# Where the softmax division stands in a windowed attention block

## What is computed

```python
s = jnp.einsum('...qhgd,...shd->...hgqs', q, k).astype(jnp.float32) * scale
s = jnp.where(mask[..., None, None, :, :], s, NEG_INF)
m = jnp.maximum(jnp.max(s, axis=-1, keepdims=True), sink)
p = jnp.exp(s - m)
denom = jnp.sum(p, axis=-1, keepdims=True) + jnp.exp(sink - m)
p = (p / denom).astype(v.dtype)
return jnp.einsum('...hgqs,...shd->...qhgd', p, v).astype(q.dtype)
```

## Time and profile before

| | us |
|---|---|
| median of 3 runs (lowest, highest) | 2438.33 (2435.63, 2440.2) |
| the profiled execution, its own time | 2430.51 |
| span of its trace | 2428.8 |
| TensorE busy | 2279.8 (94%) |
| VectorE busy | 1681.7 (69%) |
| ScalarE busy | 983.6 (40%) |
| GpSimd busy | 719.1 (30%) |

### The profile page before, as it was taken

How to read it: one execution, slowest core, us unless ns; L and a number is a source line. 1 busy time by engine, 2 the same in 40 slices (tenths; PEclk the granted TensorE clock), 3 DMA queues, 4 the chain that set the end, 5 groups by cost and what they waited for, 6 DMA issues and landing times.

```text
span 2428.8 us, 36140 instructions
## 1 busy us (share of the span) xinstructions
PE 2279.8 (94%) x14396; PEld 2034.1 (84%) x14396; DVE 1681.7 (69%) x2092; ACT 983.6 (40%) x1773; POOL 719.1 (30%) x396
## 2 busy tenths in 40 slices
PE   7999899699999999999999998987999999999997
PEld 7997577699999998887799876667999999987875
DVE  1579747777777776777536797476777777767676
ACT  3227634533443343343322366344344334443332
POOL 1110134444434440220211102344443444302201
PEclk9999889899999999999999998898999999999999
DMA  5321146122222224765552213451122222255752
GB/s 160 85 51 37 60 132 180 44 82 64 73 82 77 70 72 153 268 207 191 167 129 45 55 37 103 131 159 45 59 79 82 70 72 76 99 216 195 241 198 94
DMA packets 207975, 269.52 MB, mean 111 GB/s; under 512 B 31952, under 2 KB 166584, under 8 KB 207736
## 3 DMA queue, kind: packets, MB, share of 16 engines
q1 hardware_dynamic: 207808, 267.21, 35.9%
HBM read 217.39 MB, written 46.13 MB: 108 GB/s over the span
## 4 chain that ended last, share of the span: by engine, by line
PE 62%; DVE 17%; ACT 6%; issue 5%; POOL 4%; DMA 3%; SPq 2%; DVEq 0%; ACTq 0%; POOLq 0%
PE ps L2014 23%; PE ps L1734 18%; PE ps L1698 8%; PE ps L1956 6%; DMA wblk<-in_w_up 2%; POOL bl L716 2%; POOL wblk L724 1%; ACT bh L908 1%; SPq L529 1%; PE ps L1759 1%; DVE bl L1310 1%; DVE Sb L1524 1%; DVE bnst L1210 1%; DVE rl L1378 1%; PE ps L1853 1%
## 5 line engine op out<-in xcount | busy, mean ns | idle before, releaser
L2014 PE MATMUL ps<-bt,bh 128*128 128x272 f32 x3520 | 598.3, 293 | 29.3 <-issue 19.5
L2014 PEld LDWEIGHTS ps<-bt,bh 128*128 128x128 f32 x3520 | 503.9, 191 | 36.5 <-issue 25.2
L908 ACT ACTIVATE bh<-wblk 128x512 fp32r<-128x512 f32 x308 | 183.6, 624 | 543.1 <-POOL wblk L728 237.4
L2014 PE MATMUL ps<-bt,bl 128*128 128x272 f32 x1760 | 367.8, 291 | 0.0
L1310 DVE TENSOR_TENSOR bl<-wblk,bh 128x512 fp32r<-128x512 f32 x210 | 165.2, 804 | 183.4 <-ACT bh L908 183.4
L2014 PEld LDWEIGHTS ps<-bt,bl 128*128 128x128 f32 x1760 | 278.7, 191 | 0.0
L1734 PE MATMUL ps<-rh,ah 128*128 128x512 f32 (+1 forms) x792 | 246.3, 392 | 13.7 <-DVE rzd L1206 6.8
L716 POOL TENSOR_TENSOR bl<-wblk,bh 128x512 fp32r<-128x512 f32 x98 | 164.7, 1685 | 311.7 <-ACT bh L908 311.7
L2014 PE MATMUL ps<-ba,bh 128*128 128x272 f32 x1408 | 239.9, 293 | 9.1 <-POOL bl L716 4.1
L1734 PE MATMUL ps<-rh,al 128*128 128x512 f32 (+1 forms) x792 | 245.1, 391 | 0.0
L1734 PE MATMUL ps<-rl,ah 128*128 128x512 f32 (+1 forms) x792 | 244.4, 390 | 0.0
(11 more groups left out here) (223 smaller groups left out, 4051.5 us busy)
## 6 DMA issues: line engine op xcount, KB each, us to landing
wrow<-in_w_down SPq DMA_DIRECT2D x132, 512.0 KB, 4.3
wblk<-in_w_up SPq DMA_DIRECT2D x88, 512.0 KB, 5.2
a_scr<-hg SPq DMA_DIRECT2D x44, 552.0 KB, 3.4
araw<-a_scr SPq DMA_DIRECT2D x88, 192.0 KB, 4.1
wrow<-in_w_out SPq DMA_DIRECT2D x48, 256.0 KB, 5.3
wrow<-in_w_out SPq DMA_DIRECT2D x24, 512.0 KB, 3.5
wraw<-in_w_in SPq DMA_DIRECT2D x10, 1024.0 KB, 6.3
z_scr<-rzc SPq DMA_DIRECT2D x16, 512.0 KB, 3.6
```

The source lines that it names most:

```text
L908: act.activation(bh[b][:], block_of(f, b), ACT.Copy).then_inc(S["u_hi"], 1)
L2014: e = nc.tensor.matmul(out[:, n, :], lhs, rhs[:, HW_ // 2 * n:HW_ // 2 * n + HW_ // 2], start=(k == 0 and m == 0), stop=(k == HK - 1 and m ...
```

## The change

The probabilities stay unnormalised: L1524 is gone, `turned` waits for the exponentials alone (`a_exp`), and the product with the values is made with them as they are. The output is put right afterwards. A new function `shares(b)` on TensorE multiplies, for each of the 8 heads, the column of reciprocals (read 64 times over as the stationary operand) by the identity, so that each query's reciprocal stands on the 64 rows of its head, 128x512 in all, in PSUM bank 7. ScalarE still copies the output to `hT`, and a new `o_evac` on VectorE multiplies it there by bank 7. Since bank 7 also takes the turned values, `values_in(b)` now waits for that product of block b - 1, and has moved: it stood one block earlier, as `values_in(b + 1)`, behind the previous block's pieces. After the last block ScalarE copies the output ahead of `m_hi(l, 0)`, and TensorE's transpose of the last keys waits for the last product.

```diff
@@ ScalarE
+                o_evac(NB - 1)
                 m_hi(l, 0)
-                o_evac(NB - 1)
                 m_hi(l, 1)
@@ VectorE
                     dve.wait_ge(S["a_den"], k + 1)
+                    after(dve, "pe_r", l * NB + b)
                     dve.reciprocal(ast[:, 5, hs], ast[:, 5, hs]).then_inc(S["a_rd"], 1)
-                    dve.wait_ge(S["a_rd"], k + 1)
-                    dve.tensor_tensor(Sb[:, hs, :], Sb[:, hs, :], ast[:, 5, hs].unsqueeze(2).to_broadcast([P, 4, 2 * P]), ALU.mult)\
-                        .then_inc(S["a_nrm"], 1)
+                def o_evac(b):
+                    dve.wait_ge(S["a_o"], l * NB + b + 1)
+                    dve.wait_ge(S["pe_r"], l * NB + b + 1)
+                    o = hT[:, T_Q:T_Q + 4, b * P:b * P + P]
+                    dve.tensor_tensor(o, o, ps[:, 7, :].rearrange("p (j q) -> p j q", q=P), ALU.mult).then_inc(S["a_oev"], 1)
...
                     softmax_in(b, 1)
+                    if b:
+                        o_evac(b - 1)
                     dve.wait_ge(S["pe_vtr"], n + 1)
...
                     softmax_out(b, 1)
+                o_evac(NB - 1)
                 m_lo(l, 0)
@@ TensorE
                     after(pe, "a_vr", n)
+                    after(pe, "a_oev", n)
                     pe.transpose(ps[:, 7, 0:P], vst[:], ident[:]).then_inc(S["pe_vtr"], 1)
...
-                    pe.wait_ge(S["a_nrm"], 2 * (l * NB + b) + hf + 1)
+                    pe.wait_ge(S["a_exp"], 2 * (l * NB + b) + hf + 1)
...
-                    after(pe, "a_oev", n)
+                    after(pe, "a_o", n)
...
+                def shares(b):
+                    n = l * NB + b
+                    pe.wait_ge(S["a_rd"], 2 * n + 2)
+                    for kv in range(KV):
+                        o = 64 * kv
+                        for i in range(4):
+                            h = 4 * (i // 2) + 2 * kv + i % 2
+                            e = nc.tensor.matmul(ps[o:o + 64, 7, P * i:P * i + P], ast[:, 5, h:h + 1].to_broadcast([P, HD]), ident[:],
+                                                 start=True, stop=True)
+                    e.then_inc(S["pe_r"], 1)
...
+                    if b:
+                        values_in(b)
                     if b < NB - 1:
-                        values_in(b + 1)
                         scores(b + 1, 0)
                     turned(b, 0)
                     turned(b, 1)
                     if b < NB - 1:
                         scores(b + 1, 1)
                     values(b)
+                    shares(b)
+                pe.wait_ge(S["a_oev"], (l + 1) * NB)
                 pe.transpose(ps[:, 7, P:2 * P], kring[:, (NB - 1) % 2, :], ident[:]).then_inc(S["kv_tr"], 1)
```

More of the change, by code:

```diff
@@ L309, in trunk @@
                   "par_ev wt_tr wt_ev wt_ok wa_landed0 wa_landed1 w_hi w_lo in_done in_ev zu_ev zu_gelu gated "
-                  "g_dve g_pe g_act gv_out k_sw k_rot q_sw0 q_sw1 a_pre a_sm a_max a_m a_neg a_vr a_exp a_den a_rd a_nrm "
-                  "a_ptev a_oev pe_vtr pe_s pe_tr pe_pv kv_tr kv_ev kv_out kvc_landed s_pe s_dve s_act s_out c_out pad_ok "
+                  "g_dve g_pe g_act gv_out k_sw k_rot q_sw0 q_sw1 a_pre a_sm a_max a_m a_neg a_vr a_exp a_den a_rd pe_r "
+                  "a_ptev a_o a_oev pe_vtr pe_s pe_tr pe_pv kv_tr kv_ev kv_out kvc_landed s_pe s_dve s_act s_out c_out pad_ok "
                   "m_hi m_lo wc_landed0 wc_landed1 wc_landed2 wc_landed3 c_hused c_used c_done rz_landed0 rz_landed1 rz_landed2 "
@@ L1043, in o_evac @@
                     act.activation(hT[:, T_Q:T_Q + 4, b * P:b * P + P], ps[:, 6, :].rearrange("p (j q) -> p j q", q=P), ACT.Copy)\
-                        .then_inc(S["a_oev"], 1)
+                        .then_inc(S["a_o"], 1)
                 for b in range(NB):
```

## The result

The changed kernel takes 2490.02 us as the median of four runs (2488.28 to 2494.49), the kernel before 2436.98 beside it (2431.62 to 2440.2). The ratio is 1.0226, 95% interval 1.0214 to 1.0239: slower by 2.3%, or some 55 us. The prediction was 2492 with a range of 2474 to 2510. The profiled execution took 2490.49 us, with a span of 2488.8; before, 2430.51 and 2428.8.

A forecast was written before the change was run, and what follows sets the result against it. With TensorE's and VectorE's near-equal streams bounding the attention stage, and TensorE's path lengthened, 41.5 us for the two layers plus 12.6 for the clock made 54, taking the median from 2438.3 to 2492; range 2474 to 2510.

The forecast's parts named there:

- The bound: Attention stage: TensorE and VectorE both near their limit (97.06 and 98.41 of 112.90 us), TensorE nearly without gaps in block 1.
- The moved step: Blocks 1 to 6, both layers: scores start 2.85 us after the values' transpose starts, formerly 0.20; TensorE loses 2.65 each.
- The shares, 1.02 us a block: Eight small products on TensorE's path in every block, priced at 1.02 us from the gated MLP's eight of that form.
- The other bound: Upper price of the shares: eight full 128x128 operands at the transposes' pace, 1.09 us for four, so 2.18.
- the repeated column is slow: Rival: the shares take 2.18 us instead of 1.02, 18.6 us more in all, giving 2511; chance 0.10.
- Block 3, the transposed values behind the gelu: Layer 0: the gelu delays the output product to 235.08; the values' transpose waits, though TensorE's piece would end at 234.62.
- The end of the stage: After block 7: shares, product and m_lo add 4.5 us before the output projection; 1.7 goes with the normalisation.
- the walk: Block-by-block timing of the attention stage: +20.3 us in layer 0, +21.2 in layer 1, together +41.5.
- The clock, nine of twelve at 1.4 us: Nine of the 12 new TensorE gaps followed by a fall from 2.4 to 1.2 GHz, 1.4 us each, 12.6 together.
- The hidden round trip: Rival: input-projection pieces let VectorE run ahead, leaving only 8 x 1.02 and the longer end, 2444; chance 0.05.
- VectorE as the bound: Rival: VectorE's stream sets the stage, so 1.75 us less in each of 16 blocks gives 2410; chance 0.04.
- The clock holds: Rival: no clock falls after the new gaps, leaving the 41.5 us alone, 2480; chance 0.17.

The follow-up runs named there:

- no_norm: The kernel before without the normalising product (cut to one column of each head) and nothing in its place: 2420.00 us, ratio 0.9945.
- quarter_shares: The changed kernel with values a block ahead, alternating halves, new stage end, next queries and scores issued earlier, and two of eight shares: 2426.70 us, ratio 0.9970.
- gap_filled: The changed kernel with eight needless transposes between the transpose of the values and the next scores in blocks 1 to 6: 2479.77 us, ratio 1.0181.
- plain_column: The changed kernel with the shares' repeated column replaced by 64 ordinary columns of the identity: 2491.37 us in one run.

## Why the prediction was right, step by step

- **The bound.** Right: TensorE's stream set the stage in most blocks, so VectorE's 39 us of saved work were worth 12 to 13 (no_norm), and time added on TensorE was paid in six blocks of eight (quarter_shares). The prediction had named block 3 and the end of the stage as the places that gain; block 6, with 5.4 us the largest, it had not.
- **The moved step, 2.65 us in twelve gaps.** Right to the hundredth: 2.85 us from the transpose of the values to the scores, ten times, and in block 6 the stretch beside GpSimd, priced at 1.8 and measured at 2.02 (4.60 less 2.58).
- **The shares, 1.02 us a block.** The term that was mis-sized. At full clock a block now lasts 7.93 us from its scores to the next piece (225.81 to 233.74) instead of 6.59, so 1.34. 16 x 0.32 is 5.1 us that the sum lacked. The row of the gated MLP had the same shapes but not the same order. The other bound was read wrongly as well: the row of 1.09 us is eight transposes, not four (gap_filled's eight are recorded as x8, while eight float32 products are x16), so 1.09 and not 2.18 is the price of eight by that row. The rival "the repeated column is slow" was priced too high for that, and plain_column shows that the repeated column costs nothing.
- **Block 3, the transposed values behind the gelu, 0.46 us in each layer.** Not seen: the only waits of L1854 for L1530 are the two of block 7. The longer shares bring TensorE there later, so that the product is there first.
- **The end of the stage.** Right in kind, with the waits of 0.85 and 1.43 us ahead of the output projection (one of some 2 us was forecast). From the last scores to the output projection it was to take 24.6 us and took 27.31; 2.43 of the 2.7 are a fallen clock, which the walk had counted apart. Of the 1.7 us that were to go with the normalisation, no_norm shows 1.07.
- **The clock, nine of twelve at 1.4 us.** Eight, at 1.06 to 2.43 us, 11.8 in place of 12.6, and 10.9 without the wait in block 3. Right in sum, but with luck: nine was a choice between none and twelve, from a single row that had shown a fall once in two. gap_filled bears the size out, with 10 us for most of the falls.
- **The sum.** 41.5 for the walk, 5.1 that were missing, 11.8 for the clock: 58.4, against 58.8 in the stages. The medians differ by 53, since the profiled execution of before lies below its median and that of after on it. Had the shares been priced right, the forecast would have been 2497; the error of that term and the offset of the one profiled execution went opposite ways. The forecast of 2492 is nearer to 2490 than its terms deserve; that is luck.
- **The signs.** Twelve waits for the queries of 2.3 to 2.6 us were named: ten are 2.58, the two of block 6 are 4.60. The shares' row was to take 1.0 us and takes 1.53. The stage of layer 0 was to last 133 us and lasts 142.56; the clock (7.1 us in this layer, which the 133 left out) and the shares (2.6) are that difference.
- **The rivals.** The hidden round trip and VectorE as the bound were both wrong for the reason given against them. "The clock holds" is what gap_filled comes near to: 2479.8, where 2480 had been worked out, but with the 5.1 us of the shares in it and the clock still falling in three gaps.

## What to carry to other kernels

Before pricing what a change saves on an engine, ask what a slot that it shares (here a PSUM bank) does to the order: a transpose that had run a block ahead lost its lead to make room for small products, and that cost some three times what the saved multiplication was worth (40 to 45 us against 12 to 13). Work taken off an engine that doesn't set the pace brings only what is waited for, so leave it out in a run of its own first; had no_norm been the first step, its 13 us would have shown that a replacement of 11 to 12 us on the busier engine could hardly pay.

## What the runs showed of the chip

- Small products that write alternating 64-row halves of a bank run at 0.98 us for eight, in four-and-four order at 1.46, with the same instructions.
- Gaps of 2.58 us on TensorE were followed by half clock in six cases of ten, in the same blocks of both layers, gaps of 1.71 us with transposes ahead of them in one of ten, and a kernel with 96 needless transposes was 10 us faster for it.
- A stationary operand that repeats one column 64 times costs the same as one of 64 columns (1.46 us for eight, both).
